# Lower levels of a gated scan kept as 32x32 diagonal blocks, one matmul per block, on one Trainium2 core

## The reference

```python
def chunked_gated_scan(q, k, v, log_g):
    """S_t = diag(exp(log_g_t)) S_{t-1} + k_t^T v_t ; o_t = q_t S_t (chunkwise form)."""
    ...

def bidir_scan(q, k_f, k_b, v, lg_f, lg_b):
    flip = lambda t: jnp.flip(t, axis=2)
    o_f = chunked_gated_scan(q, k_f, v, lg_f)
    o_b = flip(chunked_gated_scan(flip(q), flip(k_b), flip(v), flip(lg_b)))
    return o_f + o_b
```

## Time and profile before

| | us |
|---|---|
| median of 3 runs | 4276.49 (4273.06 to 4277.64) |
| the profiled execution | 4283.65 |
| span of its trace | 4281.8 |
| PE busy | 3858.1 (90%) |
| DVE busy | 1958.1 (46%) |
| ACT busy | 1442.7 (34%) |

### The profile page before, as it was taken

One profiled execution on the slowest core, in us unless ns is written; L12 is line 12 of the kernel. 1 busy time (PEld: TensorE's weight loads), 2 busy tenths in 40 slices (PEclk: granted clock), 3 DMA queues, 4 the chain that ended last, 5 costly groups with the idle time before them and its releaser, 6 DMA issues.

```text
span 4281.8 us, 67153 instructions
## 1 busy us (share of the span) xinstructions
PE 3858.1 (90%) x29532; PEld 2367.6 (55%) x29532; DVE 1958.1 (46%) x2105; ACT 1442.7 (34%) x1807; POOL 989.7 (23%) x438
## 2 busy tenths in 40 slices
PE   6989999999999999998899888989788988988887
PEld 3556666666666665456544455555554455555454
DVE  3456455654554653441323255254552255254552
ACT  4222223233222312231213233454453233454452
POOL 2413323342332322031252200111002200111102
PEclk9999999999999999999999988999999988999999
DMA  2111111111111113232311200100012100100002
GB/s 97 56 36 46 39 43 56 41 51 46 53 49 41 60 46 145 96 138 99 138 64 51 80 10 11 40 23 23 25 51 84 36 10 11 36 24 20 30 24 90
DMA packets 61586, 226.95 MB, mean 53 GB/s; under 512 B 6832, under 2 KB 8560, under 8 KB 60784
## 3 DMA queue, kind: packets, MB, share of 16 engines
q1 hardware_dynamic: 52224, 189.64, 12.9%
q10 hardware_dynamic: 9072, 33.03, 1.9%
HBM read 174.93 MB, written 47.71 MB: 52 GB/s over the span
## 4 chain that ended last, share of the span: by engine, by line
PE 73%; DVE 17%; ACT 6%; DMA 2%; issue 2%; POOL 1%; DVEq 0%; SPq 0%; ACTq 0%; POOLq 0%
PE psum L1000 71%; DVE arena L2110 7%; DVE arena L2113 5%; ACT arena L1572 4%; PE psum L1003 2%; DVE arena L2502 2%; DVE arena L2568 2%; ACT wh L1572 1%; DMA arena<-in_w_proj_conv 1%; POOL hl L2627 1%; POOL arena L2627 0%; DVE arena L2117 0%; DMA arena<-in_w_in 0%; POOL wl L2627 0%; ACT arena L2044 0%
## 5 line engine op out<-in xcount | busy, mean ns | idle before, releaser
L1000 PE MATMUL psum<-arena 64*64 64x32 f32 (+12 forms) x18860 | 1452.3, 276 | 250.7 <-DVE arena L2110 89.2
L1000 PEld LDWEIGHTS psum<-arena 64*64 64x64 f32 (+6 forms) x18860 | 1045.1, 157 | 686.8 <-issue 378.6
L2627 POOL TENSOR_TENSOR wl<-arena,wh 128x1024 bf16<-128x1024 f32 (+1 forms) x203 | 493.2, 2430 | 2248.5 <-ACT wh L1572 2245.4
L1000 PE MATMUL psum<-hh,wh 128*128 128x512 f32 x3248 | 913.0, 423 | 73.3 <-ACT hh L1572 24.3
L1000 PE MATMUL psum<-hh,wl 128*128 128x512 bf16 x3248 | 825.3, 394 | 1.6 <-POOL wl L2627 1.6
L1572 ACT ACTIVATE arena<-psum 128x512 f32<-128x512 f32 (+4 forms) x660 | 415.8, 630 | 1156.7 <-PE psum L1000 856.3
L1000 PE MATMUL psum<-hl,wh 128*128 128x512 bf16 x3248 | 773.2, 384 | 8.0 <-POOL hl L2627 8.0
L1000 PEld LDWEIGHTS psum<-hh,wh 128*128 128x128 f32 x3248 | 609.5, 194 | 276.0 <-issue 50.8
L2110 DVE TENSOR_TENSOR arena<-psum,arena 128x512 f32<-128x512 f32 (+3 forms) x488 | 319.4, 654 | 894.5 <-PE psum L1000 596.6
L2113 DVE SCALAR_TENSOR_TENSOR arena<-arena 128x1024 f32<-128x1024 f32 x356 | 571.4, 1605 | 165.1 <-ACT arena L1572 148.7
L2627 POOL TENSOR_TENSOR arena<-arena 128x1024 f32<-128x1024 f32 (+4 forms) x142 | 362.2, 2550 | 869.4 <-ACT arena L1572 460.4
(11 more groups left out here) (37 smaller groups left out, 805.9 us busy)
## 6 DMA issues: line engine op xcount, KB each, us to landing
arena<-in_w_in SPq DMA_DIRECT2D x161, 512.0 KB, 3.5
scr_g<-arena ACTq DMA_DIRECT2D x24, 512.0 KB, 2.7
arena<-scr_g SPq DMA_DIRECT2D x24, 512.0 KB, 4.5
arena<-in_w_out SPq DMA_DIRECT2D x24, 512.0 KB, 3.5
arena<-in_w_mem_kv SPq DMA_DIRECT2D x16, 512.0 KB, 3.5
scr_x<-arena SPq DMA_DIRECT2D x16, 512.0 KB, 3.6
arena<-scr_x SPq DMA_DIRECT2D x16, 512.0 KB, 6.8
arena<-in_x SPq DMA_DIRECT2D x8, 512.0 KB, 10.8
```

Of the source, the lines that this page charges most:

```text
L1000: return pe.e.matmul(o, l, r, start=start, stop=stop)
L2627: return pool.seq.tensor_tensor(o, a, b, op)
```

## The change

The diagonal and levels 0 to 4 touch only 32 x 32 blocks on the diagonal of the chunks. They are now computed as such: 32 blocks of 32 tokens, for two heads, are 64 matmuls of 32 weight columns and 32 moving columns per pair of heads, the blocks going round the four column groups of the array (output partitions 0, 32, 64, 96) and the two heads on their row groups and PSUM banks. One part per pair of heads takes the place of two; it fills 256 columns in each of two banks. VectorE reads it with one COPY_PREDICATED of 128 x 512 instead of two operations of 128 x 1024 (the diagonal is now a COPY_PREDICATED too), into a compact store `blocks32`. Levels 5 and 6 go as before. After level 6 a new step `whole_at` copies the compact blocks into the full AT: four ScalarE copies per pair of heads, of 32 partitions x 512 each. `so` waits for them. `PACE` is lower because the scan has fewer yields. The host-made masks change to match.

```diff
+    mask32 = [maskf[:, 32 * i:32 * i + 32].bitcast(i32) for i in range(6)]
+    def AT16(p):
+        return cols3(AT[:, 2048 * p:2048 * p + 2048], 16)
+    def blocks32(p):
+        return BA[:, 7, 512 * p:512 * p + 512]
...
-            parts = [(g, p) for g in range(2) for p in range(nh // 2)]
-            for g, p in parts:
-                held(("diag", L, t, g, p), ("diag", L, t, g, p), room["levels"])
+            for p in range(nh // 2):
+                held(("diag", L, t, p), ("diag", L, t, p), room["levels"])
...
                 do("xk", L, t, lv)
                 yield
+                parts = [(g, p) for g in range(1 if lv < 5 else 2) for p in range(nh // 2)]
                 for g, p in parts:
...
+            do("whole_at", L, t)
             for d in range(2):
                 for g in range(2):
                     one(("kt", L, t, d, g), ("kt", L, t, d, g), LOWER)
...
-    PACE = (0.62, 0.59, 0.555, 0.555)
+    PACE = (0.565, 0.535, 0.505, 0.505)
...
+        def bank32(use, j):
+            return pair(use)[:, 512 * j:512 * j + 256]
...
-            for c in range(4 * g, 4 * g + 4):
+            for n in range(32):
+                b, o, cc = slice(32 * (n % 4), 32 * (n % 4) + 32), slice(32 * (n // 4), 32 * (n // 4) + 32), slice(32 * n, 32 * n + 32)
                 for j in range(2):
                     r = slice(dk * (2 * p + j), dk * (2 * p + j) + dk)
-                    x = mm(head(use, j)[:, c % 4, :], ks[r, cc], qq[r, cc])
+                    x = mm(bank32(use, j)[b, o], ks[r, cc], qq[r, cc])
...
+            if lv < 5:
+                for n in range(32):
+                    b, o, cc = slice(32 * (n % 4), 32 * (n % 4) + 32), slice(32 * (n // 4), 32 * (n // 4) + 32), slice(32 * n, 32 * n + 32)
+                    for j in range(2):
+                        r = slice(dk * (2 * p + j), dk * (2 * p + j) + dk)
+                        q = QF[1][r, cc]
+                        qv = bass.AP(q.tensor, q.offset, [list(q.ap[0]), [2 * m, 16 // m], [1024 + m, 2], [1, m]])
+                        x = mm(bank32(use, j)[b, o], (ks, qq)[lv % 2][r, cc], qv)
+                x.then_inc(*pe.up(*use))
+                return
...
                 pe.wait_ge(*at("carry", L, t, 1))
+                pe.wait_ge(*at("AT", L, t, p))
...
+        def whole_at(L, t):
+            for p in range(2 if t == 0 else 1):
+                act.wait_ge(*at("ATl", "lev", L, t, 6, 1, p))
+                for b in range(4):
+                    s = slice(32 * b, 32 * b + 32)
+                    f(AT16(p)[s, :, s], cols3(blocks32(p), 16)[s], AF.Copy).then_inc(*(act.up("AT", L, t, p) if b == 3 else act.up("AT", L, t, p, b)))
...
+        def in32(o, mask, use):
+            i = pair(use).rearrange("p (j n) -> p j n", j=2)[:, :, 0:256].rearrange("p j (c t) -> p j c t", t=32)
+            m = mask.unsqueeze(1).unsqueeze(1).to_broadcast([128, 2, 8, 32])
+            return dve.seq.copy_predicated(o.rearrange("p (j c t) -> p j c t", j=2, t=32), m, i)
...
-            tt(AT8(p, g), cols3(pair(use), 8), ident.unsqueeze(1).to_broadcast([128, 8, 128]), MUL).then_inc(*dve.up("AT0", *use))
+            if t:
+                dve.wait_ge(*at("AT", L, t - 1, 1 if t == 1 else 0))
+            in32(blocks32(p), mask32[0], use).then_inc(*dve.up("AT0", *use))
...
+            if lv < 5:
+                in32(blocks32(p), mask32[lv + 1], use).then_inc(*dve.up("ATl", *use))
+            else:
+                m = masks[lv].unsqueeze(1).unsqueeze(1).to_broadcast([128, 2, 4, 128])
+                i = pair(use).rearrange("p (j c t) -> p j c t", j=2, t=128)
+                dve.seq.copy_predicated(AT8(p, g), m, i).then_inc(*dve.up("ATl", *use))
```

More of the change, by code:

```diff
@@ L278, in build @@
     F0 = T2 + 3712
-    masks = [maskf[:, 128 * i:128 * i + 128].bitcast(i32) for i in range(8)]
+    mask32 = [maskf[:, 32 * i:32 * i + 32].bitcast(i32) for i in range(6)]
+    masks = {lv: maskf[:, 128 * lv + 128:128 * lv + 256].bitcast(i32) for lv in (5, 6)}
     XR = BC
@@ L749, in scan @@
                 yield
-                do("diage", L, t, g, p)
-                ps.leave(("diag", L, t, g, p))
+                do("diage", L, t, p)
+                ps.leave(("diag", L, t, p))
             for step in gate:
@@ L940, in build @@
             ("small", "x_load x_store consts2 small_load small mix_load xr_load store"),
-            ("scan", "sv_copy sv_turn sq_copy sk_copy ga_copy ga_up ga_z ga_abs ga_ln ga_min ga_exp hz_gate hz_f ks diag diage qf xk lev leve grow kt st so"
+            ("scan", "sv_copy sv_turn sq_copy sk_copy ga_copy ga_up ga_z ga_abs ga_ln ga_min ga_exp hz_gate hz_f ks diag diage qf xk lev leve whole_at grow kt st so"
                      " so_copy so_sum so_rs so_norm sg_sig sg_out"),
@@ L1354, in heads, with diag @@
             return (4, 32) if t == 0 else (2, 64)
+        def bank32(use, j):
+            return pair(use)[:, 512 * j:512 * j + 256]
         def head(use, x):
             return cols3(pair(use)[:, 512 * x:512 * x + 512], 4)
-        def diag(L, t, g, p):
+        def diag(L, t, p):
             nh, dk = heads(t)
-            use = ("diag", L, t, g, p)
+            use = ("diag", L, t, p)
             cleared(use)
@@ L1962, in xk @@
             if lv == 0:
-                act.wait_ge(*at("diag", L, t, 1, 1 if t == 0 else 0))
+                act.wait_ge(*at("diag", L, t, 1 if t == 0 else 0))
                 act.wait_ge(*at("qf_dve", L, t))
@@ L1967, in xk @@
                 if lv > 1:
[L1968 removed]
+                    act.wait_ge(*at("lev", L, t, lv - 2, 0, 1 if t == 0 else 0))
                 act.wait_ge(*at("grow_k", L, t, lv - 1, 1))
@@ L2093, in scalar_program @@
                     mt=mt, close=close, small=small, sv_copy=sv_copy, sv_turn=sv_turn, sq_copy=sq_copy, sk_copy=sk_copy,
-                    ga_copy=ga_copy, ga_abs=ga_abs, ga_ln=ga_ln, ga_exp=ga_exp, hz_gate=hz_gate, xk=xk, kt=kt, so_copy=so_copy, so_rs=so_rs,
+                    ga_copy=ga_copy, ga_abs=ga_abs, ga_ln=ga_ln, ga_exp=ga_exp, hz_gate=hz_gate, xk=xk, whole_at=whole_at, kt=kt, so_copy=so_copy, so_rs=so_rs,
                     sg_sig=sg_sig, dv_copy=dv_copy, dv_turn=dv_turn, dq_copy=dq_copy, dexp=dexp, e1=e1, WT=WT_, do=do_, do_sq=do_sq,
@@ L2508, in grow @@
             dve.wait_ge(*at("xk", L, t, lv))
-            dve.wait_ge(*at("lev", L, t, lv, 1, 1 if t == 0 else 0))
+            dve.wait_ge(*at("lev", L, t, lv, 0 if lv < 5 else 1, 1 if t == 0 else 0))
             m = 1 << lv
@@ L2921, in constants @@
     a, b = p[:, None], p[None]
-    mk[:, 0:128] = a == b
-    for i in range(7):
+    for i in (5, 6):
         m = 1 << i
         mk[:, 128 * i + 128:128 * i + 256] = (a // (2 * m) == b // (2 * m)) & (a // m != b // m)
+    a, b = a % 32, np.arange(32)[None]
+    mk[:, 0:32] = a == b
+    for i in range(5):
+        m = 1 << i
+        mk[:, 32 * i + 32:32 * i + 64] = (a // (2 * m) == b // (2 * m)) & (a // m != b // m)
     return c1, np.ascontiguousarray(c2.astype(np.float32)), mk
```

13 lines of the change are left out of this document (5 added, 8 removed).

## The result

The changed kernel takes 4257.19 us (median of 5 runs, 4253.66 to 4261.89) against 4276.49 us for the kernel before beside it (median of 5 runs, 4273.06 to 4284.02): a ratio of 0.9955, 95% interval 0.9941 to 0.9970. It is 19 us faster, not the 88 of the forecast. Its profiled execution took 4253.66 us. Each ratio is uncertain by about 0.0015, so a difference between two kernels that were timed on different occasions is known to about 9 us only.

What follows compares the result with a forecast made beforehand. TensorE was taken to bound the kernel, though not everywhere by its work, with idle time and lost clock in the level stretches. Terms -56 - 20 - 33 + 21 = -88 us gave 4196 us profiled, 4189 median; range 4118 to 4286.

Steps and rivals of the forecast that it cites:

- VectorE: Diagonal products and masked copies: 168.5 us of work becomes 80.7, 88 us less, none of it kernel time by itself.
- TensorE's own work: Diagonal and five levels: 48 units at 1.5 us instead of 2.18, -33 us; ends -55 and +81.
- The count-bound rival: Small matmuls bound by their count at 30.2 ns per record, 3.87 us a unit: 4302 us, slower; chance 0.15.
- The rule of 25 ns or 60 cycles per matmul: Cost of each small matmul on TensorE: 128 records would take 3.2 us per unit, +49 us instead of -33.
- The waits that the masked copies feed: TensorE's waits on COPY_PREDICATED in the level stretches shrink and clock returns: -56 us; bounds -20 and -110.
- the knock-on: A shorter VectorE queue lets attention row minima, grow and carries through sooner: -20 us, between 0 and -45.
- ScalarE's copies: Compact-block copies ahead of the kt copies delay TensorE 3.5 us in each of six scans: +21 us; ends +5, +35.
- Pace: The scan has 24 fewer yields per layer and the pace falls 9%, so it ends where it did: no term.
- the length of a small part: Profile sign on TensorE: a part of 128 records takes 1.0 to 2.1 us at full clock.
- the waits on masked copies: Profile sign: TensorE's waits on COPY_PREDICATED in the mixes come near 27 us instead of 57.6.
- the clock in the GLA stretches: Profile sign: TensorE's granted clock in the GLA stretches rises above 0.85.
- The rival of the renamed stall: The level chain is late as often as the PSUM pair, so waits change name: -5 us, 4271 us; chance 0.11.

Runs made afterwards that it cites:

- the halved matmuls: Kernel before with half the matmuls of the diagonal and levels 0 to 4 left out: ratio 0.9895, -45 us; TensorE's busy time fell by 60 us.
- the runs with swapped paces: Changed kernel with the old pace: 0.9986, 13 us slower than the changed kernel; kernel before with the new pace: 1.0091, 39 us slower than before.
- the doubled kernel: Changed kernel with each small matmul issued twice into the same place: ratio 1.0355 to the kernel before, 171 us over the changed kernel.

## Why the prediction was wrong

The direction was right and the sum was not: -88 forecast, -19 measured. By its steps:

- *VectorE.* The 128x512 masked copy takes 0.73 us, between the two ends, below the 0.796 taken; 168.5 us became 77.8, 91 less where 88 were forecast. VectorE's total fell by 63 only, since its other operations got slower on the whole: the 128x512 products from SBUF take 761 ns on average instead of 705, the 128x1024 scaled ones 1642 instead of 1605, while the plain 128x1024 products got faster, 1377 instead of 1434. What changed them was not tested.
- *TensorE's own work*, -33: mis-sized. The shape was judged well (1.5 us taken, 1.39 found), but the parts it replaces were priced at full clock, 2.18 us a pair; they took 2 x 1.37, since part of them ran at the low clock. The busy time fell by 65 us. At the three quarters that the halved matmuls gave, that is an estimate of -49.
- *The instruction supply*, not in the sum: pauses of 13 us in this kernel's trace, 7 to 24 us in its variants that keep the parts whole. The count-bound rival had the right suspicion, that so many instructions in a row stand nowhere in the trace, and the wrong mechanism: a record costs 9.5 ns (1.21 us for 128), less than the earlier trace rows show, and the price is paid by the page. The rule of 25 ns or 60 cycles per matmul that the prediction cites from the Trainium skill does not agree with the trace, and its +49 us did not come.
- *The waits that the masked copies feed*, -56, *and the knock-on*, -20: the step that failed. It read the waits on L2502 as time that the shorter and fewer copies would return. At the changed levels they did shrink, from 44.7 to 12.5 us; but the sum of TensorE's waits rose, from 234 us to between 255 and 265, with more of them on ScalarE and on the unchanged levels' copies. Half-width copies in the old plan returned 25 us for 48, so 91 us might have returned some 45 (an estimate). With the pauses at 13 us, -49 + 13 + 23 = -13 without any such gain, and 19 were measured, so about 6 us of it arrived; with the pauses at 24 it would be 17. Some 30 to 40 us are missing. What failed is that the sum left the other waits as they were, because they belong to the chain from level to level, "which the change does not shorten". The change did not lengthen the chain either. It took two of four parts, and two of six yields, out of each GLA level's round (one of two parts and one of four yields in HGRN), and TensorE now comes to the level's matmuls before ScalarE's key copies are there (38 us of waits in front of the small matmuls, 16 before). Moving one yield in between brings 17 us back, adding as many as were removed 38. That much the runs show; that the removed parts are what had covered this wait is the likely reading, and stays open.
- *ScalarE's copies*, +21: right, 23 measured. That another place costs less was not thought of.
- *Pace*, "no term": right as far as the total goes, as the runs with swapped paces show. But the pace keeps the whole scan in step, not each link, and the loss lay in a link.

Of what was to be seen in the profile, the count and length of the masked copies, the length of a small part and the eight groups of ScalarE copies came as said; the waits on masked copies went to 42 us, not 27; the clock in the GLA stretches reached 0.85 and was not above it, and it fell in the stretch behind.

The rival of the renamed stall, at 0.11, came nearest to what happened, and its 4271 was closer than the forecast. It is right that the waits return under ScalarE's name. It had TensorE's work at 6 us, far too small. The range from 4118 to 4286 held the time.

What stays open: the terms above are each measured in a kernel of its own and need not add, and the pauses differ between variants (7 to 16 waits on issue, 7 to 24 us, in those with whole parts and whole traces). Whether another order of the small matmuls avoids them without the loss of slack was not tried.

## What to carry to other kernels

When a plan is written out by hand, a removed step takes its place in the order with it: after a cut, ask of every link of a chain whether the work that still stands in it is enough, and look first at whether the total of the waits fell or only the name beside them. Price work that goes away by the clock at which it ran, not by the best example of it. And a long run of very small matmuls can have a cost that none of its records shows, the fetching of its instructions.

## What the runs showed of the hardware

- Small float32 matmuls of 32 weight columns and 32 moving columns spread over two row groups and four column groups, with 32 or 64 rows of weights, go at 1.21 to 1.22 us for 64 of them at the full clock, from their start to the start of the next work, 19 ns each.
- TensorE runs dry on dense small matmuls: in the doubled kernel 61 pauses for 109 us, most of them 1.5 to 2.1 us long, 128 matmul records apart where the run goes on, and 56 of them ending 1.2 to 1.6 us after a 16 KB packet of the instruction queue has landed. Thinning the same work to half a page at a time removed most of them in the changed kernel (4.1 us left).
- A packet of the instruction queue holds 256 instructions: 12288 more of them took 48 packets more.
- A ScalarE copy of 32 partitions x 512 takes 0.66 us, no less than one of 128 partitions (0.643).
